# Passage from the second phase to attention reordered, and the stores of q, k and v issued from ScalarE's queue

## The reference

```
# layer 0: norm, GLU, causal depthwise convolution of width 31, LayerNorm, gate, projection, residual
a, gl, z = split(rms_norm(x, g_norm) @ w_in, 3)
v = a * sigmoid(gl)
c = depthwise_conv(concat(prefix, v), w_dw) + b_dw
x = x + (silu(layer_norm(c)) * silu(z)) @ w_out
# shared keys and values, once
k, v = split(rms_norm(x, g_kv) @ w_kv); k = rms_norm_per_head(k)
# layer 1: window of 128, 16 query heads on 4 key heads, sinks, linear distance penalty
q, z = split(rms_norm(x, g_norm) @ w_in_b); q = rms_norm_per_head(q)
o = softmax_with_sink(q k^T / 8 - slope * dist) v
y = x + (o * silu(z)) @ w_out_b
```

## Time and profile before

| | |
|---|---|
| median of 3 runs | 1884.6 us (1883.93 to 1886.74) |
| profiled execution | 1884.13 us, span 1882.3 us |
| mean granted TensorE clock | 0.969 |
| busy: PE, PEld, DVE, ACT, POOL | 93%, 76%, 64%, 45%, 31% |
| DMA, mean | 98 GB/s |

### The profile page before, as it was taken

How to read it: one execution, slowest core, us unless ns; L and a number is a source line. 1 busy time by engine, 2 the same in 40 slices (tenths; PEclk the granted TensorE clock), 3 DMA queues, 4 the chain that set the end, 5 groups by cost and what they waited for, 6 DMA issues and landing times.

```text
span 1882.3 us, 25336 instructions
## 1 busy us (share of the span) xinstructions
PE 1748.9 (93%) x9105; PEld 1421.9 (76%) x9105; DVE 1199.6 (64%) x2013; ACT 848.6 (45%) x1658; POOL 590.9 (31%) x446
## 2 busy tenths in 40 slices
PE   7999999999997377999999999779999999999998
PEld 6798988888886356787888887557777777777776
DVE  6378889898997445785666643345555556655553
ACT  5555655555563352232323232345444554445442
POOL 2399999999993002221121211100000000000000
PEclk9999999999999588999999999979999999999999
DMA  6221211111212545334444432552221232222311
GB/s 200 81 73 39 73 37 51 57 44 61 64 39 100 167 137 202 137 109 123 137 134 131 148 124 100 175 162 87 82 87 64 76 107 72 93 71 82 101 49 40
DMA packets 157228, 184.47 MB, mean 98 GB/s; under 512 B 55189, under 2 KB 120829, under 8 KB 152972
## 3 DMA queue, kind: packets, MB, share of 16 engines
q1 hardware_dynamic: 157116, 183.00, 30.0%
HBM read 115.31 MB, written 70.34 MB: 99 GB/s over the span
## 4 chain that ended last, share of the span: by engine, by line
PE 54%; DMA 5%; DVE 3%; ACT 2%; SPq 1%; issue 1%; POOL 1%; DVEq 0%; ACTq 0%; POOLq 0%
PE c_acc L119 19%; PE b_pso L119 12%; PE b_psq L119 9%; PE c_pss L1937 3%; PE c_psp L1946 3%; PE c_pso L1961 3%; DMA ht_d<-b_ht 1%; PE b_pst L1248 1%; DVE b_x L1114 1%; PE c_pso L1955 1%; PE b_psc L1242 1%; PE c_pst L1868 1%; DMA b_cz<-in_w_in_b 1%; PE c_pss L119 1%; DMA b_three<-v_left 1%
## 5 line engine op out<-in xcount | busy, mean ns | idle before, releaser
L687 PE MATMUL a_ps<-a_xt,a_wring 128*128 128x512 f32 (+3 forms) x2880 | 556.4, 354 | 13.6 <-ACT a_zo L509 9.3
L687 PEld LDWEIGHTS a_ps<-a_xt,a_wring 128*128 128x128 f32 x2880 | 494.3, 189 | 70.3 <-ACT a_zo L509 11.4
L446 POOL TENSOR_TENSOR a_csum<-a_prod,a_csum 128x704 f32<-128x704 f32 (+1 forms) x242 | 425.5, 1758 | 42.9 <-ACT a_prod L496 7.5
L588 DVE SCALAR_TENSOR_TENSOR a_pst<-a_vbuf,taps,a_pst 128x704 f32<-128x704 f32 (+1 forms) x352 | 327.6, 931 | 11.0
L496 ACT ACTIVATE a_prod<-a_vbuf,taps 128x704 f32<-128x704 f32 (+1 forms) x264 | 225.7, 865 | 182.5 <-POOL a_csum L446 168.5
L119 PE MATMUL b_pso<-w,b_yt 128*128 128x512 f32 (+1 forms) x816 | 193.1, 396 | 0.3 <-DVE b_yt L1108 0.3
L119 PE MATMUL c_acc<-w,c_ht 128*128 128x512 f32 x768 | 185.9, 398 | 0.2 <-issue 0.2
L119 PEld LDWEIGHTS b_pso<-w,b_yt 128*128 128x128 f32 (+1 forms) x816 | 151.7, 188 | 35.3 <-DVE b_yt L1108 0.7
L119 PE MATMUL c_acc<-w,c_ot 128*128 128x512 f32 x720 | 172.0, 394 | 0.0
L119 PEld LDWEIGHTS c_acc<-w,c_ht 128*128 128x128 f32 x768 | 143.3, 190 | 36.5 <-issue 7.3
L119 PEld LDWEIGHTS c_acc<-w,c_ot 128*128 128x128 f32 x720 | 132.9, 188 | 32.5 <-issue 5.8
(11 more groups left out here) (182 smaller groups left out, 2158.7 us busy)
## 6 DMA issues: line engine op xcount, KB each, us to landing
ht_d<-b_ht SPq DMA_DIRECT2D x16, 1024.0 KB, 4.7
c_ht<-ht_d SPq DMA_DIRECT2D x16, 1024.0 KB, 4.8
a_stage<-in_w_in_a SPq DMA_DIRECT2D x24, 512.0 KB, 4.0
a_x<-in_x_prompt SPq DMA_DIRECT2D x16, 512.0 KB, 3.4
b_cz<-c_d SPq DMA_DIRECT2D x16, 512.0 KB, 4.9
b_cz<-z_d SPq DMA_DIRECT2D x16, 512.0 KB, 6.7
b_x<-in_x_prompt SPq DMA_DIRECT2D x16, 512.0 KB, 3.5
x_d<-b_x SPq DMA_DIRECT2D x16, 512.0 KB, 2.6
```

The lines of the kernel that those rows point to most:

```text
L446: pool.tensor_tensor(out, prod[:, (PTAPS * n + i) % RING, 0:t1 - t0], out, ALU.add).then_inc(prod_added, 1)
L588: dve.scalar_tensor_tensor(part if k == DTAPS - 1 else here, vbuf[:, b % 2, t0 + k:t1 + k], wcol(k, b), part if k == 0 else here, ALU.mult ...
L687: last = pe.matmul(out, wring[:, u % 3, a, k], xt[c][:, e, k, 0:n], start=(k == 0 and a == 0 and e == 0), stop=(k == KT - 1 and a == 1))
```

## The change

Phase b's q, k and v of tiles 0 to 14 are stored by ScalarE's queue, each in the list of the tile two later, between `silu_z` and `square_x1`; SyncE's list of a tile ends with its loads. Tiles 15 and 16 are stored by SyncE after the last tile, in pieces between weight loads. The gate's weights go through four stages in another place. SyncE, ScalarE, VectorE and PE are given new lists for the passage: the five splits stand before `cut_h(16)` as they did, but the queries of tile 15 behind it; PE turns q and k of attention's tile 0 between the keys' and the queries' projection of tile 16, and ScalarE copies them (`turned`) before the last six splits. Sixteen small stores of the decode tile's k and v become two copies from DRAM to DRAM. Six pieces of the output weights are loaded ahead of the last q store and not four. The weights of keys and values take slot 4 (whose place c_qt and c_kt share) and those of the second half of the queries slot 2; `kvo` and the left-over window change places in `b_three`; small buffers of phase c move; q's scale is made at the start of phase b.

```diff
-    OUT0, OUT1, KVS, Q0, Q1 = range(5)
+    OUT0, OUT1, Q1, Q0, KVS = range(5)
...
-    kvo = early_stage[:, 2, 0:2 * KV]
+    kvo = early_stage[:, 0, 0:2 * KV]
...
-    gate_stage = cz[:, 0:w.stages * HALF].rearrange("p (s n) -> p s n", s=w.stages)
+    gate_stage = nc.alloc_sbuf_tensor_at("b_gate", [P, 4, HALF], F32, offset=g.w_base + 4 * g.slot_bytes + p.at["three"] + 4 * HALF)
...
+            if isinstance(t, int) and t == TILES:
+                sp.wait_ge(ht_out, 16 * (TILES - 1))
...
             if isinstance(t, int) and t == TILES:
-                sp.wait_ge(tc_done, ALL)
-                sp.wait_ge(prod_ready, ALL)
-                w.stage = gate_stage
-                split_weights_dma(sp, io.w_in_b[:, D:D + HALF], w, 3)
-            if not (isinstance(t, int) and t == 0):
-                store_qkv(t - 1)
+                return
+
...
         steady(sp, body, all_convolved)
-        split_weights_dma(sp, io.w_in_b[:, D + HALF:2 * D], w, 4, k1=w.stages)
-        sp.wait_ge(ht_out, 16 * TILES)
-        sp.wait_ge(q_out, 16 * TILES)
-        sp.wait_ge(kv_out, 16 * TILES)
+        sp.wait_ge(tc_done, ALL)
+        sp.wait_ge(prod_ready, ALL)
+        gates(0, 4)
         sp.wait_ge(x1_out, 16 * ALL)
+        sp.wait_ge(h_ready, ALL)
+        sp.wait_ge(kv_out, 16 * (TILES - 1))
+        sp.wait_ge(q_out, 16 * (TILES - 1))
+        load_queries()
+        store_kvq(TILES - 1)
+        sp.dma_start(io.k_p, kvo[:, 0:KV]).then_inc(copy_out, 16)
+        sp.dma_start(io.v_p, kvo[:, KV:2 * KV]).then_inc(copy_out, 16)
+        gates(4, 8)
         sp.wait_ge(th_done, ALL)
-        first_loads()
-        split_weights_dma(sp, io.w_in_b[:, D + HALF:2 * D], w, 4, k0=w.stages)
+        load_keys()
         store_ht(ALL - 1)
-        p.store_last = lambda: store_qkv(ALL - 1)
+        gates(8, 12)
+        load_rest()
+        store_q(TILES - 1)
+        gates(12, 16)
+        store_kvq(ALL - 1)
+        sp.wait_ge(kv_out, 16 * ALL)
+        for to, cols in ((io.k_s, slice(0, KV)), (io.v_s, slice(KV, 2 * KV))):
+            sp.dma_start(to[:, P - DS:P, :], g.kv_d[SEQ:TOK, cols].rearrange("(b i) n -> b i n", b=DB)).then_inc(copy_out, 16)
+        p.store_last = lambda: store_q(ALL - 1)
...
+        def store_kvq(t):
+            act.wait_ge(k_ready, t + 1)
+            act.wait_ge(v_ready, t + 1)
+            act.dma_start(token_rows(g.kv_d, t, P), kvo[:, :]).then_inc(kv_out, 16)
+            act.wait_ge(q_ready, t + 1)
+            act.dma_start(token_rows(g.q_d, t, P), qo[:, :]).then_inc(q_out, 16)
...
+            if not (isinstance(t, int) and t < 2):
+                store_kvq(t - 2)
             if not start:
                 square_x1(t)
...
         steady(act, body)
+        act.wait_ge(out_mm, ALL)
+        gates(0, 5)
         cut_h(ALL - 1)
-        split_weights_hi(act, 0, gains[Q0], w, 3, k0=5)
-        split_weights_hi(act, 1, gains[Q0], w, 4, k1=w.stages)
+        queries(TILES - 1)
+        gates(5, 10)
         keys_values(ALL - 1)
-        split_weights_hi(act, 1, gains[Q0], w, 4, k0=w.stages)
+        turned()
+        gates(10, 16)
         queries(ALL - 1)
...
         steady(dve, body)
+        gates(0, 5)
         cut_h(ALL - 1)
-        queries(ALL - 2)
-        split_weights_lo(dve, 0, gains[Q0], w, 3, k0=5)
-        split_weights_lo(dve, 1, gains[Q0], w, 4, k1=w.stages)
+        query_sums(TILES - 1)
+        gates(5, 8)
+        queries(TILES - 1)
+        gates(8, 10)
         keys(ALL - 1)
-        split_weights_lo(dve, 1, gains[Q0], w, 4, k0=w.stages)
+        gates(10, 16)
         query_sums(ALL - 1)
...
             project(pe, ps_o[0:n, 0:HALF], ht, w.wslot[KVS], n, (w.w_lo, 0) if gate else None).then_inc(kv_mm, 1)
+            if between is not None:
+                between()
             after(pe, q_ready, t)
...
+        def load_rest():
             sp.dma_start(dist[:, 0:2 * P], io.distance).then_inc(tab_in, 16)
             sp.dma_start(dist[:, 2 * P:3 * P], io.distance[:, 0:P]).then_inc(tab_in, 16)
+            sp.dma_start(sink0[:, :], io.sinks.broadcast_to([P, HEADS])).then_inc(tab_in, 16)
+            load_ht(0)
             load_v(0, 0)
...
-        split_weights_dma(sp, io.w_out_b[:, 0:HALF], w, 0, k1=w.stages)
+        w.stage = stg
+        split_weights_dma(sp, io.w_out_b[:, 0:HALF], w, 2, k1=6)
         prev.store_last()
         sp.wait_ge(prev.q_out, 16 * ALL)
-        sp.wait_ge(prev.kv_out, 16 * ALL)
-        sp.wait_ge(prev.w.w_lo, 5 * KT)
+        sp.wait_ge(w.w_lo, 2 * KT)
...
+            if first:
+                split_weights_dma(sp, io.w_out_b[:, 0:HALF], w, 2, k0=6)
             if not last:
                 load_q(t + 1)
                 load_k(t + 1, 1 - r)
             if first:
-                split_weights_dma(sp, io.w_out_b[:, 0:HALF], w, 0, k0=w.stages)
                 load_v(1, 1)
+                split_weights_dma(sp, io.w_out_b[:, HALF:D], w, 3, k1=4)
                 load_ht(1)
-                split_weights_dma(sp, io.w_out_b[:, HALF:D], w, 1)
+                split_weights_dma(sp, io.w_out_b[:, HALF:D], w, 3, k0=4)
...
+        def turned():
+            act.wait_ge(prev.qscale_made, 1)
+            queries(0)
+            keys(0, 0)
...
+        def first_turns():
+            turn_q(0)
+            turn_k(0, 0)
```

More of the change, by code:

```diff
@@ L751, in phase_b @@
     cd = conv[:, 2 * DB * (HIST + DS):].rearrange("p (a n) -> p a n", a=2)
-    vw = early_stage[:, 0:2].rearrange("p a n -> p (a n)")[:, 0:LEFT1 - LEFT0 + HIST]
+    vw = early_stage[:, 1:3].rearrange("p a n -> p (a n)")[:, 0:LEFT1 - LEFT0 + HIST]
     cw = conv[:, 0:LEFT1 - LEFT0]
     gains = {KVS: g.cols[:, KT:2 * KT], Q0: g.cols[:, 2 * KT:3 * KT], Q1: g.cols[:, 2 * KT:3 * KT]}
+    p.gain, p.gate_stage = gains[Q0], gate_stage
     kgain = sb("b_kgain", [P, HD])
+    p.qscale = sb("b_qscale", [P, 1])
     stats = sb("b_stats", [P, 2, 6])
@@ L846, in store_qkv, with store_q @@
             sp.dma_start(token_rows(g.kv_d, t, n), kvo[0:n]).then_inc(kv_out, 16)
[L847 to L854, removed]
+            if not (isinstance(t, int) and t >= TILES - 1):
+                store_q(t)
+        def store_q(t):
+            n = rows_of(t)
             sp.wait_ge(q_ready, t + 1)
@@ L1065, in body @@
                 split_weights_hi(act, Q0, gains[Q0], w, 1)
+            if isinstance(t, int) and t == TILES:
+                return
             if not (isinstance(t, int) and t == 0):
                 queries(t - 1)
-        w.stage = early_stage
         silu_z(0)
@@ L1217, in body @@
                 if isinstance(t, int) and t == TILES:
-                    w.stage = gate_stage
-                    split_weights_lo(dve, 0, gains[Q0], w, 3, k1=5)
+                    return
                 query_sums(t - 1)
+        dve.tensor_scalar(p.qscale[:, :], g.qgain[:, :], HD ** -0.5, None, ALU.mult).then_inc(qscale_made, 1)
         normalize(0)
-        w.stage = early_stage
         gate(0)
@@ L1268, in out, with qkv @@
             ins.then_inc(out_mm, 1)
-        def qkv(t, gate=False):
+        def qkv(t, gate=False, between=None):
             n = rows_of(t)
@@ L1294, in tensor @@
         steady(pe, body)
-        qkv(ALL - 1)
+        qkv(ALL - 1, between=between)
     p.w, p.ht_out, p.x1_out, p.q_out, p.kv_out, p.copy_out = w, ht_out, x1_out, q_out, kv_out, copy_out
@@ L1329, in phase_c @@
     otd = at("c_otd", [P, 2, KT, DEC], prev.at["qo"], F32R)
-    small = [prev.at["three"]]
+    small = [prev.at["cz"] + 6144 + 3 * P * 4]
     def sb(name, shape):
@@ L1339, in phase_c @@
     nsink = sb("c_nsink", [P, HEADS])
+    small[0] = prev.at["three"] + 4 * HALF
     sinkd = sb("c_sinkd", [P, 2])
@@ L1353, in phase_c @@
     knt = sb("c_knt", [P, 2, DEC])
-    kdt = at("c_kdt", [P, 2, DK], prev.at["three"] + 2 * 4 * HALF)
+    kdt = at("c_kdt", [P, 2, DK], prev.at["three"])
     szd = at("c_szd", [P, KT, DEC], prev.at["cz"])
@@ L1607, in decode_cut, with gates @@
             act.activation(otd[:, 0], szd[:, :, :], ACT.Copy).then_inc(d_act, 1)
-        prev.scalar(act)
-        act.wait_ge(nsink_made, 1)
-        queries(0)
-        keys(0, 0)
+        def gates(first, stop):
+            w.stage = prev.gate_stage
+            for k in range(first, stop):
+                split_weights_hi(act, Z0 + k // KT, prev.gain, w, k // KT, k0=k % KT, k1=k % KT + 1)
+        def turned():
+            act.wait_ge(prev.qscale_made, 1)
+            queries(0)
+            keys(0, 0)
+        prev.scalar(act, gates, turned)
+        w.stage = stg
         def body(t, r):
@@ L1619, in body @@
             first = isinstance(t, int) and t == 0
-            split = lambda k: split_weights_hi(act, OUT0 + k // KT, 0.5, w, k // KT, k0=k % KT, k1=k % KT + 2) if first else None
+            split = lambda k: split_weights_hi(act, OUT0 + k // KT, 0.5, w, 2 + k // KT, k0=k % KT, k1=k % KT + 2) if first else None
             if not first:
@@ L1781, in decode_cut, with gates @@
```

(17 more changed lines are left out.)

43 lines of the change are left out of this document (18 added, 25 removed).

## The result

| | before | after |
|---|---|---|
| median of the runs beside each other | 1885.67 us | 1857.53 us |
| profiled execution, span | 1884.13, 1882.3 us | 1857.53, 1855.7 us |
| mean granted TensorE clock | 0.969 | 0.978 |
| busy PE | 1748.9 us, 93% | 1740.1 us, 94% |

The ratio is 0.9852, with an interval of 0.9835 to 0.9869: by it 27.9 us faster (28.1 between the two medians). Forecast were 1859 us and a range of 1850 to 1873.

The account below looks back on a forecast made before the run. PE, busy 93%, was taken as the bound, with time won only at its waits or low clock. 1884.1 less 12.6 (moved stores) and 13 (passage) gave 1858.5, plus 0.5 for the median: 1859 us, range 1850 to 1873.

Parts of the forecast that it names:

- The bound: PE is busy 93%; time is won only where it waits or clocks low: start of second phase and passage to attention.
- Tiles 4 and 6: Second phase: left-over convolution loads no longer blocked behind SyncE's wait for q; gains of 3.8 and 5.8 us.
- Rival (a): The convolution's loads are late for their own sake, so moving the stores gives nothing: 1871.6 us; chance 9%.
- 7.3 us chain: Tile 6's convolution chain (store, landing, four loads), cited for the first rival with a margin of only 3.1 us.
- Tile 2: Second phase: left-over load issued some 1.7 us earlier, without 768 KB of stores ahead; 3.0 us of the 8.09 wait go.
- ScalarE's queue: Two issues and two waits added ahead of `square_x1`, up to 0.47 us per issue, hidden by 6.5 us of cover.
- rival (d): Slower: stores hold ScalarE's in-order queue, so `silu_y` and the keys slip; 1904 us; chance 4%.
- The passage: From second phase to attention: new lists shorten PE's waits, 15.6 us at `pv(1)` less 1.8 and some 1: 13 us.
- The first projection of the 64-row tile: Passage start: earlier `cut_h(16)` shrinks the 2.32 us wait by 1.0; the projection goes from 7.30 back to 5.7 us.
- The copy stands before the last six splits: ScalarE copies attention tile 0's transposes earlier; scores start at 1213.9, where PE had waited 8.70 us to 1225.23.
- the sixteen small stores: Passage: SyncE spent 1224.70 to 1231.18 on these stores of k and v; now they are two.
- Rival (b): The passage is limited by transfers, at a DMA share of 0.68, and gains only 4 us: 1868 us; chance 15%.

Follow-up runs that it names:

- stores-only run: Kernel before, with only q, k and v of tiles 0 to 14 stored from ScalarE's queue, passage as it was: 1874.9 us, ratio 0.9949.
- late copies: Kernel after, with the two 960 KB cache-to-output copies issued in tile 7, not tile 0, of the second phase: 1849.8 us, ratio 0.9817.
- passage alone: Kernel after, with the stores of q, k and v of tiles 0 to 14 back at the end of SyncE's tile lists: 1868.1 us, ratio 0.9911.
- late transposes: Kernel after, with attention's first transposes behind the last tile's queries and their copies behind all splits: 1857.7 us, ratio 0.9852.
- small stores: Kernel after, with the decode tile's sixteen k and v stores back behind the output-weight loads, replacing the two DRAM copies: 1863.4 us, ratio 0.9881.
- split behind: Kernel after, with the first pair of output-weight splits behind the first key head's exponentials and their sums, SyncE's list unchanged: 1863.6 us, ratio 0.9886.
- stores moved within SyncE's list: Kernel after, with the q, k, v stores in SyncE's queue behind the left-over stores and loads, none from ScalarE: 1857.4 us, ratio 0.9858.
- four pieces ahead: Kernel after, with four pieces of output weights, not six, loaded ahead of the last q store: 1869.5 us, ratio 0.9916.
- both mended: Kernel with late copies, first pair of output splits behind exponentials and gate, SyncE's list four pieces, last q store, other four, decode loads: 1850.3 us.

## Why the prediction was right, and where not

**The bound.** Right: PE's waits at those two places carried the change, and no steady tile moved (30.7 to 30.8 us throughout).

**Tiles 4 and 6.** Right in mechanism and size: 9.7 us for 9.6. SyncE's rows in after carry the chain: the second left-over load is issued at 784.52 (forecast about 784.5), and tile 6's chain starts at 845.40 and has its loads issued by 851.07. VectorE waits for neither.

```profile
784.52 0.43 SPq L891 DMA_DIRECT2D b_three<-v_left  x1
...
845.40 0.36 SPq L871 DMA_DIRECT2D c_d<-b_conv  x1
848.25 0.63 SPq L861 DMA_DIRECT2D b_conv<-hist_d  x1
848.92 0.72 SPq L862 DMA_DIRECT2D b_conv<-vnew_d  x1
...
850.40 0.67 SPq L862 DMA_DIRECT2D b_conv<-vnew_d  x1
```

Rival (a) fell with the stores-only run. (Its "7.3 us chain" does not agree with the "about 7 us" of the sum; in the old trace SyncE began the chain at 858.24, so it took 6.9.)

**Tile 2.** Wrong: 3.0 us were forecast, 0.8 came in PE's start of the transposes (735.72 to 734.96), and the 24 matmuls behind took 7.65 instead of 6.83 (granted clock 0.73 and 0.82), so nothing stayed. The failed step is "no longer has 768 KB of stores ahead of it, which I put at 1 to 2 us": the load was issued 1.3 us earlier and not 1.7, and without those stores ahead it took 6.8 us and not less than the 6.3 before. I read only what stood before the load, and not what had put the whole tile late, two stores (ht and x) behind two copies. The run with late copies shows it: tile 2 lasts 30.7 us there, 40.2 before the change, and 39.6 to 41.7 in the eight profiles with the stores moved and the copies early.

**ScalarE's queue.** Right, and rival (d) fell. The issues take 0.34 us each in a steady tile of after (0.40 and 0.49 in tile 2), in an idle time of 11.03 us that did not change (11.05 in the earlier trace rows):

```profile
823.88 0.34 ACTq L1054 DMA_DIRECT2D q_d<-b_qo  x1
830.39 1.06 ACT L1018 ACTIVATE b_qo<-b_x 128x1024 f32<-128x1024 f32 x1 [11.03 <-DVE b_x L1136]
```

In tile 2 the landing of the first q store held `square_x1` to 736.40, as foreseen and off PE's path. But the queue itself gained nothing either, which the prediction left unsaid.

**The passage.** The sum was 13 us, measured are 17.2. The moments came out close once the 9.9 us that lie ahead of the passage are taken off: scores at 1204.0 (measured 1204.08), `turn_p(0)` at 1215.1 (1215.91), the fourth pair issued at 1221.5 (1222.10), `pv(1)` at 1227.3 (1227.89). The term that was mis-sized is what I took off behind `pv(1)`: 1.8 for the clock and 1 for rounding. The low clock came as forecast, but it cost nothing: PE waited 0.56 there and not 3, since the slow second gate projection (8.01 us) filled the time. Five profiles with the same or nearly the same lists show it: that projection took 7.32 to 8.01 us and the wait 1.57 to 0.56, and the two together always 8.5 to 8.9. The clock was back behind it: 5.75 us for the decode's projection that had taken 7.33. 15.0 at `pv(1)`, 1.6 from that projection, and small things make 17.2.

**The first projection of the 64-row tile.** 1.41 us of waiting instead of 2.32, and 5.73 instead of 7.30 us: as forecast, but by luck. With the passage alone, late transposes, small stores and the split behind, the same wait of 1.41 was followed by 7.3 us. The luck is worth little at the end: from the start of this projection to `pv(1)` it is 41.6 to 42.1 us with the fast one (after, stores moved within SyncE's list, late copies) and 42.3 and 42.0 with the slow one (passage alone, late transposes), since ScalarE's and SyncE's chain runs beside PE.

**Reasons that the runs do not bear out.** "The copy stands before the last six splits" was my reason for the scores: undoing the early copies costs 0.2 us, which is nothing by this measurement. What ended that wait is that the splits themselves end earlier: the last of the sixteen ended 27.4 us after the start of the last transposes of h before the change and 19.9 after it. With at most three loads on their way it is 30.2, and 9.8 us are lost. So the fourth is needed; that it is enough without the new order of SyncE's list was not run. And I charged the sixteen small stores with 6.5 us of SyncE's time before the change; there they cost 0.4, because q was not ready. They would cost 5.9 now. Six pieces ahead of the q store carry the second half of the passage. The rest of the new order of SyncE's list was not run by itself, and its share is not shown.

**Rival (b)**, transfers as the limit of the passage, fell by its number, 4 us for the measured 17.2. The share of 0.68 was no ceiling: in the first 21 us of the passage the 16 engines are busy for 0.75 both before and after (235 GB/s in both), and over the whole of it the share rose from 0.56 to 0.64 and the rate from 170 to 194 GB/s. The first line is before, from 1193, the second after, from 1183:

```profile
1193.00:1214.00 21.00, 18.68 (x81) 10.83 (x80) 8.30 (x12) 5.93 (x10) 4.33 (x4) 0.92 0.75 235
1183.00:1204.00 21.00, 19.59 (x97) 11.98 (x95) 11.30 (x18) 10.79 (x17) 5.14 (x4) 1.00 0.75 235
```

**Total.** 1859 against 1857.5: 3 too much in tile 2 and 4 too little in the passage, so two errors of opposite sign made the total better than its parts. That it came within 1.5 us is luck.

## What to carry to other kernels

A queue that only issues transfers is a list in order: for each of its waits, read what stands behind it, not only what it waits for. The length of the wait says little: SyncE's 122.0 us of waiting for q cost nothing once the left-over loads stood ahead of them. Moving the blocked item to another place in the same list did as much as a second queue. When a wait has been taken away, follow the list of issues that waits for the moved work before counting the gain: twice here the later loads took back all that was won, once with 6 us more.

## What had not been expected of the hardware

Two copies from DRAM to DRAM of 960 KB each, issued at 706.93 and 707.74, let the next store (1 MB) release ScalarE only 14.7 us after its issue; the stores of ht land in 3.9 us in the median of the same trace. In the kernel with late copies the median of the two stores of ht in that stretch is 5.6 us, and 11.6 with the copies early.

After a wait of 1.41 us at the same place, 24 matmuls took 5.73 us, at a granted clock of 1.00 (2.4 GHz), in five profiles (after, stores moved within SyncE's list, four pieces ahead, late copies, both mended) and 7.30 to 7.32, at a mean granted clock of 0.76 to 0.77 (in part at the lower level, 1.2 GHz), in four (passage alone, late transposes, small stores, split behind). PE's list ahead of it was the same. What decides it stays open. It is 1.6 us at that place, of which some 0.3 was left at `pv(1)` in the mean (two profiles against three, above).
